# Opening in halves with identity transposes in between, token halves normed on their own load, and moved places in the per-engine step tables

## The reference, cut to what matters

```python
def swiglu(h, w_gate, w_up, w_down):
    return (jax.nn.silu(h @ w_gate) * (h @ w_up)) @ w_down

for l in range(DEPTH):          # first_block, DEPTH = 2
    f = swiglu(rms_norm(h, ffn1_pre_g[l]), ffn1_w_gate[l], ffn1_w_up[l], ffn1_w_down[l])
    h = h + 0.5 * rms_norm(f, ffn1_post_g[l])
    u = rms_norm(h, mix_pre_g[l])
    ...                         # u @ w_in, two convolutions, two attentions (C and D), gates
    h = h + rms_norm(merged @ w_o[l], mix_post_g[l])
    ...                         # second feed-forward net
for l in range(DEPTH):          # second_block
    h = hybrid_layer(h, ...)    # norm, u @ w_in, three attentions, gates, h + o @ w_out
return rms_norm_2(h, final_g)
```

## Time and profile before

| | us |
|---|---|
| median of three runs | 1720.66 |
| the profiled execution, its own time | 1720.55 |
| its span | 1718.8 |
| TensorE (PE) busy | 1657.5 (96%) |
| VectorE (DVE) busy | 1091.5 (64%) |
| ScalarE (ACT) busy | 806.2 (47%) |
| GpSimd (POOL) busy | 36.9 (2%) |
| TensorE idle in 0 to 50 | 13.8 |
| TensorE idle in 300 to 400 | 4.8 |
| TensorE idle in 1400 to 1500 | 9.6 |

### The profile page before, as it was taken

One profiled execution on the slowest core, in us unless ns is written; L12 is line 12 of the kernel. 1 busy time (PEld: TensorE's weight loads), 2 busy tenths in 40 slices (PEclk: granted clock), 3 DMA queues, 4 the chain that ended last, 5 costly groups with the idle time before them and its releaser, 6 DMA issues.

```text
span 1718.8 us, 25141 instructions
## 1 busy us (share of the span) xinstructions
PE 1657.5 (96%) x10644; PEld 1489.9 (87%) x10644; DVE 1091.5 (64%) x1269; ACT 806.2 (47%) x1071; POOL 36.9 (2%) x60
## 2 busy tenths in 40 slices
PE   6999999999999999999999999999999998899897
PEld 6999899978889999899998997788899997778776
DVE  4544578898666454655456798875754556665664
ACT  5343544555545433444345355444543446554653
POOL 0000000000000000000000000000000000000000
PEclk9999999999999999999999999999999999999999
DMA  7555454444545555555546545345555545224321
GB/s 281 189 179 197 172 220 172 166 158 148 183 179 199 194 179 189 174 203 194 182 162 221 196 170 174 131 166 194 212 187 184 193 147 163 74 91 153 118 74 49
DMA packets 54479, 292.92 MB, mean 170 GB/s; under 512 B 5712, under 2 KB 10208, under 8 KB 27232
## 3 DMA queue, kind: packets, MB, share of 16 engines
q1 hardware_dynamic: 50880, 278.94, 46.0%
q10 hardware_dynamic: 3488, 12.38, 2.0%
HBM read 290.23 MB, written 1.06 MB: 169 GB/s over the span
## 4 chain that ended last, share of the span: by engine, by line
PE 80%; DVE 9%; ACT 5%; DVEq 3%; issue 2%; DMA 1%; POOL 0%; ACTq 0%; SPq 0%; POOLq 0%
PE ps L1542 23%; PE ps L1544 23%; PE ps L1543 23%; DVE wlo L1021 3%; ACT whi L674 2%; PE ps L2005 2%; DVEq L1303 1%; DVE mix L1212 1%; PE ps L2031 1%; DMA raw<-stream 1%; PE ps L1640 1%; DVEq L1217 1%; ACT tmp L677 1%; DVE small L1304 1%; PE ps L1685 1%
## 5 line engine op out<-in xcount | busy, mean ns | idle before, releaser
L1021 DVE TENSOR_TENSOR wlo<-raw,whi 128x2048 fp32r<-128x2048 f32 (+2 forms) x270 | 603.6, 2242 | 381.3 <-ACT whi L674 372.8
L1542 PE MATMUL ps<-xhi,whi 128*128 128x256 f32 (+1 forms) x2000 | 570.1, 285 | 0.0
L1544 PE MATMUL ps<-xhi,wlo 128*128 128x256 f32 (+1 forms) x2000 | 565.8, 283 | 0.0
L1543 PE MATMUL ps<-xlo,whi 128*128 128x256 f32 (+1 forms) x2000 | 565.8, 283 | 0.0
L674 ACT ACTIVATE whi<-raw 128x2048 fp32r<-128x2048 f32 (+2 forms) x270 | 498.6, 1868 | 18.9 <-DMA raw<-stream 16.6
L1542 PEld LDWEIGHTS ps<-xhi,whi 128*128 128x128 f32 (+1 forms) x2000 | 381.9, 191 | 4.5 <-issue 0.9
L1543 PEld LDWEIGHTS ps<-xlo,whi 128*128 128x128 f32 (+1 forms) x2000 | 382.0, 191 | 3.1
L1544 PEld LDWEIGHTS ps<-xhi,wlo 128*128 128x128 f32 (+1 forms) x2000 | 381.9, 191 | 0.5
L1542 PE MATMUL ps<-whi,yar 128*128 128x512 f32 x620 | 245.6, 396 | 3.1 <-DVE yar L1529 1.6
L1543 PE MATMUL ps<-wlo,yar 128*128 128x512 f32 x620 | 241.4, 389 | 0.0
L1544 PE MATMUL ps<-whi,yar 128*128 128x512 f32 x620 | 241.0, 389 | 0.0
(11 more groups left out here) (213 smaller groups left out, 1347.3 us busy)
## 6 DMA issues: line engine op xcount, KB each, us to landing
raw<-stream SPq DMA_DIRECT2D x210, 1024.0 KB, 4.8
raw<-stream SPq DMA_DIRECT2D x88, 512.0 KB, 4.6
raw<-stream SPq DMA_DIRECT2D x22, 384.0 KB, 3.8
gpre<-pre_gain ACTq DMA_DIRECT2D x9, 512.0 KB, 4.1
gpost<-post_gain ACTq DMA_DIRECT2D x6, 512.0 KB, 5.4
mix<-cum ACTq DMA_DIRECT2D x2, 1024.0 KB, 4.7
raw<-stream SPq DMA_DIRECT2D x4, 320.0 KB, 4.3
h<-x_in SPq DMA_DIRECT2D x2, 512.0 KB, 5.9
```

The source lines that it names most:

```text
L1021: TT(wlo[:, s, 0:w], raw[:, s, 0:w], whi[:, s, 0:w].bitcast(F32), ALU.subtract).then_inc(lo_v, 1)
L1542: pe.matmul(dst, lh, rh, start=first, stop=False)
L1543: pe.matmul(dst, lh, rl, start=False, stop=False)
L1544: return pe.matmul(dst, ll, rh, start=False, stop=last)
```

## The change

In the opening: SP loads x half 0, the gain, x half 1, and chunk 0 in two halves of 1024 columns, each with a semaphore. The gain is no longer on ScalarE's queue, so the identity is first there. ScalarE and VectorE split chunk 0 by halves; ScalarE writes `xhi` of token half 0 between the two halves and that of token half 1 before it splits chunk 1; VectorE splits chunk 1 only after all four `low`. VectorE waits for each token half's own load. ScalarE issues the loads of `gpost` and of the other constants after `split(2)`. TensorE runs 18 identity transposes into bank 3 (which nothing reads) ahead of `turns(0, 0)` and 9 behind it, and `first_pair` takes the place of `token_pair` for chunks 0 and 1: the same 96 matmuls, chunk 0 first for both token halves, then chunk 1, with waits on halves.

In the tables some places are moved. Sorted, the lists change in these ways. Mixer, ScalarE: `split` 32 before `flip` 2, `split` 33 before `turn` 7 (each was behind it). Mixer, VectorE: `scores` 2 before `split` 20, and `conv` (17, 1) between the two, `weigh` 2 before `split` 21, `scores` 3 before `split` 22, `weigh` 5 and `values` 4 before `split` 27, `split` 29 behind `weigh` 6, `values` 5, `o_split` 1 and `conv` 27, `split` 30 behind `scores` 7. Mixer, TensorE: the same order as before. Hybrid, TensorE: `flip` 1 before chunk 6, `scores` 9 before `turn` 8. Hybrid, ScalarE: `split` 5 before `l_square`, `split` 6 and `l_hi` before `take` (3, 0), `split` 10 behind `o_copy` 1 (it was before `a_square`), `split` 11 behind the two `flip_copy`, `exp` 2 before `split` 12, `split` 13 before `o_copy` 4 and gate 0, `split` 14 before `o_high` 0. Hybrid, VectorE: `split` 4 before `l_norm`, `split` 5 before `l_lo`, `weigh` 6 and `split` 13 before `o_low` 0.

```diff
--- before.py
+++ after.py
@@ -162,6 +162,7 @@
 
 LANDED = landed_counts()
 GROUPS1 = 8
+WARM = 18
 
 
 COLS_V = (2, 3, 6, 7)
@@ -185,14 +186,14 @@
-    at(pe, (17.02, 19.04, 21.04, 23.04, 25.06, 27.04, 29.04, 31.04), "scores")
+    at(pe, (17.02, 19.04, 21.04, 23.04, 25.06, 27.04, 29.04, 31.3996), "scores")
-             31.55, 32.55, 33.55, 34.55, 35.55, 36.55, 37.55, 38.55, 39.55, 40.55, 41.55, 42.55, 43.55, 44.55, 45.55,
+             31.55, 31.7404, 32.55, 34.55, 35.55, 36.55, 37.55, 38.55, 39.55, 40.55, 41.55, 42.55, 43.55, 44.55, 45.55,
@@ -209,7 +210,7 @@
-             16.55, 17.55, 18.55, 19.55, 20.55, 21.55, 22.55, 23.55, 24.55, 25.55, 26.55, 27.55, 28.55, 29.55, 30.55,
+             16.55, 17.55, 18.55, 19.55, 21.05, 22.05, 23.05, 23.55, 24.55, 25.55, 26.55, 28.057, 28.55, 30.55, 31.0601,
@@ -218,7 +219,7 @@
-             19.06, 20.06, 21.06, 22.06, 23.06, 24.06, 24.1, 25.1, 25.5275, 26.08, 28.14, 29.08, 30.12, 31.08, 32.12,
+             19.06, 20.06, 21.0447, 22.06, 23.06, 24.06, 24.1, 25.1, 25.5275, 26.08, 28.14, 29.08, 30.12, 31.08, 32.12,
@@ -276,22 +277,22 @@
-    at(pe, (6.02, 6.52, 6.54, 6.56, 9.02, 9.04, 10.52, 10.54), "flip")
+    at(pe, (6.02, 6.2376, 6.54, 6.56, 9.02, 9.04, 10.52, 10.54), "flip")
-    at(pe, (7.52, 8.52, 9.5539, 10.02, 10.56, 11.02, 12.02, 12.52, 14.02, 14.52), "turn")
+    at(pe, (7.52, 8.52, 9.5539, 10.02, 10.56, 11.02, 12.02, 12.52, 14.0607, 14.52), "turn")
-    at(act, (0.91, 1.91, 2.91, 3.91, 4.6801, 5.91, 6.91, 7.91, 8.91, 9.0669, 10.91, 11.91, 12.91, 13.91, 14.4), "split", range(3, 18))
-    at(act, (1.4, 1.9, 3.4, 3.9, 4.4, 4.5105, 5.4, 5.9, 7.4, 7.9, 9.4, 9.9), "take", TAKES)
+    at(act, (0.91, 1.9031, 1.91, 2.91, 4.6801, 5.91, 6.91, 8.91, 9.0669, 9.2882, 10.91, 11.3652, 12.91, 13.91, 14.4), "split", range(3, 18))
+    at(act, (1.4, 1.9, 3.9, 4.0105, 4.0985, 4.2, 5.2, 5.7, 7.4, 7.9, 9.4, 9.9), "take", TAKES)
-    at(act, (6.6, 7.56, 9.08, 9.56, 10.06, 10.6, 11.06, 12.06, 12.56, 14.06), "exp")
-    at(act, (7.52, 8.52, 9.52, 10.02, 10.56, 11.02, 12.02, 12.52, 14.02, 14.52), "copy")
-    at(act, (7.58, 8.54, 9.58, 10.08, 10.62, 11.08, 12.08, 12.58, 14.08, 14.54), "o_copy")
+    at(act, (6.6, 7.56, 9.08, 9.56, 10.06, 10.6, 11.36, 12.06, 12.56, 14.06), "exp")
+    at(act, (7.52, 8.52, 9.52, 10.02, 10.56, 11.32, 12.02, 12.52, 14.02, 14.52), "copy")
+    at(act, (7.58, 8.54, 9.58, 10.08, 10.92, 11.38, 12.08, 12.58, 14.08, 14.54), "o_copy")
-    at(act, (10.9, 11.9, 12.9, 13.9), "gate")
-    at(act, (11.069, 13.52, 15.02), "o_high")
-    at(dve, (1.52, 2.56, 3.54, 4.52, 6.06, 7.12, 8.1, 9.06, 9.6, 10.64, 11.52, 12.6, 13.54, 14.56, 16.3), "split", range(3, 18))
+    at(act, (11.2, 11.9, 12.9, 13.9), "gate")
+    at(act, (11.369, 13.52, 15.02), "o_high")
+    at(dve, (1.52, 2.5325, 2.56, 3.54, 5.76, 7.12, 8.1, 9.06, 9.6, 10.64, 11.52, 12.6, 13.54, 14.56, 16.3), "split", range(3, 18))
@@ -304,7 +305,7 @@
-    at(dve, (11.11, 13.53, 15.03), "o_low")
+    at(dve, (11.7636, 13.53, 15.03), "o_low")
@@ -440,6 +441,9 @@
 
         landed = [sem(f"landed{i}") for i in range(SLOTS)]
         hi_ready = sem("hi_ready")
+        first_in = sem("first_in")
+        hi_half = sem("hi_half")
+        lo_half = sem("lo_half")
         lo_v = sem("lo_v")
         used = sem("used")
         cst_in_s = sem("cst_in")
@@ -598,9 +602,13 @@
         @block.sync
         def _(sp):
 
-            for t in range(NT):
-                sp.dma_start(h[:, t, :], x_in[t]).then_inc(x_in_s[t], 16)
-            for c in range(STREAM_CH):
+            sp.dma_start(h[:, 0, :], x_in[0]).then_inc(x_in_s[0], 16)
+            sp.dma_start(gpre[:, :], pre_gain[0].partition_broadcast(P)).then_inc(gpre_in, 16)
+            sp.dma_start(h[:, 1, :], x_in[1]).then_inc(x_in_s[1], 16)
+            for half in range(2):
+                cut = slice(half * CW // 2, (half + 1) * CW // 2)
+                sp.dma_start(raw[:, 0, cut], stream[LOAD[0]][:, cut]).then_inc((first_in, landed[0])[half], 16)
+            for c in range(1, STREAM_CH):
                 if c >= SLOTS:
                     sp.wait_ge(used, c - SLOTS + 1)
                 s, w = c % SLOTS, chunk_width(c)
@@ -755,19 +763,22 @@
                     hidden(g)
                     split(c + 4)
 
-            act.dma_start(gpre[:, :], pre_gain[0].partition_broadcast(P)).then_inc(gpre_in, 16)
             act.dma_start(cst[:, 0:P], cst_in[:, 0:P]).then_inc(ident_in, 16)
             for t in range(NT):
                 act.wait_ge(x_in_s[t], 16)
                 for n in range(2):
                     square(h[:, t, n * 512:(n + 1) * 512], t, n, 2)
+            for half in range(2):
+                cut = slice(half * CW // 2, (half + 1) * CW // 2)
+                if half:
+                    turned(0, 0)
+                act.wait_ge((first_in, landed[0])[half], 16)
+                A(whi[:, 0, cut], raw[:, 0, cut], ACT.Copy).then_inc((hi_half, hi_ready)[half], 1)
+            turned(0, 1)
+            split(1)
+            split(2)
             act.dma_start(gpost[:, :], post_gain[0].partition_broadcast(P)).then_inc(gpost_in, 16)
             act.dma_start(cst[:, P:CST2], cst_in[:, P:CST2]).then_inc(cst_in_s, 16)
-            split(0)
-            split(1)
-            turned(0, 0)
-            turned(0, 1)
-            split(2)
             act.dma_start(gpre[:, :], pre_gain[1].partition_broadcast(P)).then_inc(gpre_in, 16)
 
             for l in range(DEPTH):
@@ -1120,14 +1131,17 @@
                 mean_square(2 * t + 2, t, 2)
                 if t == 0:
                     dve.wait_ge(gpre_in, 16)
-                    dve.wait_ge(x_in_s[0], 16)
-                    dve.wait_ge(x_in_s[1], 16)
+                dve.wait_ge(x_in_s[t], 16)
                 normed(t, t + 1)
-            split(0)
-            split(1)
+            for half in range(2):
+                cut = slice(half * CW // 2, (half + 1) * CW // 2)
+                dve.wait_ge((hi_half, hi_ready)[half], 1)
+                TT(wlo[:, 0, cut], raw[:, 0, cut], whi[:, 0, cut].bitcast(F32),
+                   ALU.subtract).then_inc((lo_half, lo_v)[half], 1)
             for t in range(NT):
                 low(0, t, 0)
                 low(0, t, 1)
+            split(1)
             split(2)
 
             for l in range(DEPTH):
@@ -1695,9 +1709,40 @@
                         if t:
                             ins.then_inc(used, 1)
 
+            def first_part(c, t, part, x, ks, waits=()):
+
+                for w in waits:
+                    pe.wait_ge(*w)
+                for k in ks:
+                    ins = pe.matmul(ps[:, c, t * GF:(t + 1) * GF], x[:, k, t * P:(t + 1) * P],
+                                    part[:, c, k * GF:(k + 1) * GF], start=(part is whi and x is xhi and k == 0),
+                                    stop=(x is xlo and k == KD - 1))
+                return ins
+
+            def first_pair():
+
+                low_k, high_k, all_k = range(4), range(4, KD), range(KD)
+                first_part(0, 0, whi, xhi, low_k, [(hi_half, 1), (xhi_done, 1)])
+                first_part(0, 0, whi, xhi, high_k, [(hi_ready, 1), (xhi_done, 2)])
+                turns(0, 1)
+                first_part(0, 0, wlo, xhi, low_k, [(lo_half, 1)])
+                first_part(0, 0, wlo, xhi, high_k, [(lo_v, 1)])
+                first_part(0, 0, whi, xlo, all_k, [(x_ready, 2)])
+                first_part(0, 1, whi, xhi, all_k, [(xhi_done, 4)])
+                first_part(0, 1, wlo, xhi, all_k)
+                first_part(0, 1, whi, xlo, all_k, [(x_ready, 4)]).then_inc(used, 1)
+                for t in range(NT):
+                    first_part(1, t, whi, xhi, all_k, [(hi_ready, 2)])
+                    first_part(1, t, wlo, xhi, all_k, [(lo_v, 2)])
+                    ins = first_part(1, t, whi, xlo, all_k)
+                ins.then_inc(used, 1)
+
             def ffn(ch, f, X):
 
-                token_pair(ch, X, GF)
+                if X:
+                    token_pair(ch, X, GF)
+                else:
+                    first_pair()
                 ready(ch + 2)
                 pe.wait_ge(silu_done, f * NG + 1)
                 features(ch + 2, 0)
@@ -1736,7 +1781,11 @@
 
             pe.wait_ge(setup, 1)
             pe.wait_ge(ident_in, 16)
+            for n in range(WARM):
+                pe.transpose(bank(3)[:, 0:P], ident, ident)
             turns(0, 0)
+            for n in range(WARM // 2):
+                pe.transpose(bank(3)[:, 0:P], ident, ident)
             for l in range(DEPTH):
                 ch = layer1(l)
                 ffn(ch + AT_FFN1, l * 2, l * 3)
```

## The result

The changed kernel takes 1700.8 us (median of 4 runs, 1700.3 to 1702.94) against 1721.88 for the one before (4 runs, 1720.39 to 1725.74): a ratio of 0.9877, 95% interval 0.9857 to 0.9896, 21.1 us faster. The forecast was 1699.5, range 1694 to 1708. The profiled execution took 1700.73, its span is 1698.9 (1718.8 before).

The account below looks back on a forecast made before the run. The prediction took TensorE, busy 1657.5 of 1718.8 us, as the bound, so only its idle time and slow stretches counted. Seven terms summed to 21.05 us off the 1720.55 profiled, giving 1699.5 us, range 1694 to 1708.

Parts of the forecast that it names:

- forecast case: Whole kernel: the time comes as summed, 1699.5 us, its own range 1696 to 1703; chance 0.47.
- opening: Kernel start: chunk 2's product starts at 24.9 instead of 31.06, 6.1 us won.
- mixers: Both mixer layers: TensorE's waits for weigh 2, values 3 and values 6 shrink or go, 4.05 us won.
- hybrid head: Start of both hybrid layers: new 1.2 us wait at l_turn, outweighed by waits removed at the flips; 0.45 us won.
- values 1, flip 5 (a_square): Hybrid layers: split 10 no longer precedes a_square, so waits of 1.52 and 2.35 become 0.9 and 1.2; 3.5 us won.
- slowed clock behind flip 5: Hybrid layers: shorter waits leave TensorE's clock up in the slow stretches; 3.1 us won, between nothing and 5.1.
- splits 13 and 14: Hybrid layers: these splits go ahead of the gates, removing waits of 0.57 and 1.04; 3.2 us won.
- scores 9: Hybrid layers: scores 9 before turn 8 removes the 0.33 wait before the output products; 0.65 us won.
- The sum's side of the question: Opening: the sum has identity transposes warm TensorE's clock, with the higher level from 12 on.
- that rival: The lower clock stays: transposes do not warm (2.1 less), slow stretches remain (3.1 less), or both; 1701.6 to 1704.7, chance 0.25.
- the last rival: Opening and first net: the new order holds TensorE's clock down, making the kernel slower, 1727 us; chance 0.03.
- VectorE is the mixer's bound: Mixer: what turn 2 wins is waited for at turn 4 and the flips; 1702.7 us, chance 0.10.

Follow-up runs that it names:

- v3_early: The changed kernel with weigh 4 and values 3 moved ahead of a split in VectorE's mixer table; 1701.9 us (median of 4 runs).
- head_back: The changed kernel with the hybrid layer's head (splits 4 to 6, takes 2 to 7, flip 1) in the order of before; 1698.99 us (one run).
- fill_all: The changed kernel with identity transposes in five of TensorE's waits, in the mixer and hybrid layers; 1700.07 us (median of four runs).
- fill_entry: The changed kernel with 20 more identity transposes in TensorE's wait at the first hybrid layer's entry; 1699.37 us (median of 4 runs).

## Why the prediction was right

The forecast case came, 1.3 us from the median. The terms, as the prediction summed them and as the two traces give them:

```
term                            predicted   traces
opening                              6.1      5.7
mixers                               4.05     5.6
hybrid head                          0.45    -1.3
values 1, flip 5 (a_square)          3.5      4.0
slowed clock behind flip 5           3.1      2.2
splits 13 and 14                     3.2      1.5
scores 9                             0.65     1.15
not the change's                              1.1
sum                                 21.05    20.0
```

*The opening.* By its steps: the identity landed at 4.90 (estimated 5.1). x half 1 came later than kept: its square is at 8.28, not 7.79. Each step behind it on ScalarE is later by the same 0.5: the half split started at 9.89 for 9.4, both `xhi` ended at 12.06 for 11.5, the second half split at 13.0 for 12.5. That is as much as the term lacks.

*The clock there.* The sum's side of the question was right and the rule's wrong; its price, 2.1 in that rival, measured 0.95. (The longest stretch at the lower level before was 6.8 us, at 1479, not the 6.4 of the last rival; nothing hangs on it.)

*The mixers.* Turn 4 starts 1.81 and 1.78 earlier for the 1.85 said, by VectorE's idle time, as the step had it. The term behind it was mis-sized: 0.40 for turn 7's wait, 1.0 measured, since turn 5's wait of 0.20 went too, and a wait costs somewhat more than it shows. "VectorE is the mixer's bound" is now true of the next step: v3_early got nothing.

*The hybrid head.* This is the step that failed, by its sign. The new wait of 1.2 at `l_turn` came as worked out (1.19), and flip 0's 1.02 went. But in the first layer TensorE loses 1.61 up to `l_turn`, 0.4 more than the wait shows, and wins only 0.99 back up to flip 0. What the step left out is ScalarE's take (L946) ahead of the chunk behind the flips, now later: a wait of 0.55 at 1434.67, for the 0.34 that went. head_back confirms 1.05 of the 1.3. "Flip 1 finds its input" was right and worth nothing.

*a_square, flip 5.* 2.2 and 1.8 where 1.75 was said; values 1's wait fell to 1.11, not 0.9, and flip 5's to 0.60, not 1.2.

*The slowed stretches.* Right for the first layer (nothing behind flip 5) and wrong for the second, where 1.7 us are lacking from 1607 on in spite of the shorter waits. Whether a stretch comes is not settled by the wait's length, as the table above shows; a term that counts on one going can only be a chance.

*Splits 13 and 14.* The 0.57 and 1.04 went, and were half replaced: turn 7 now waits 1.04 for VectorE's weigh, which stood just behind. The step had asked for no next bound.

So the mechanisms are mostly those forecast, but that the total came so near is in part luck: four terms are too high (4.75 together), three too low (2.55), and 1.1 us no term had, 0.84 of it a late chunk in the profiled execution of before. The two profiled executions themselves differ by 19.8, the medians by 21.1.

## What to carry to other kernels

A saturated engine carries what the opening wins to the end, and in the opening the place of the small copies in a queue of long splits was worth more (4.6 of 5.7 us, up to 1.7 of it by the clock) than loading in halves or warming the clock (0.25 and 0.95). Ask of each removed wait what else reaches that point: at turn 4, 2.2 us of it were worth nothing, and at `l_turn` a wait hid the landing of a chunk that cost 1.86 once it stood bare. Where one engine idles often for a microsecond or two, compare traces instruction by instruction before reading a median: stretches of lower clock, worth 0.5 (fill_all) to 1.5 us (fill_entry) each here, come and go with unrelated edits.

## What was not expected of the hardware

Identity transposes brought TensorE's clock to its upper level (0.22 to 0.12 us apart, in the opening after 4.7 us of nothing else). Where 20 of them filled a gap of 2.35 us it stayed up in three traces of three; without them it fell in nine of eleven. The lower-clock stretches come in one size, 1.7 us of full clock lacking, or double, and the same wait of 2.2 to 2.7 us brings one in some kernels' traces and none in others. In the opening itself the profile's granted clock reads 1.00 while matmuls run at the spacing of the lower level, so there only the spacing tells.

The head of before with fill_entry's transposes would, by an estimate from single traces (1698.99 less the 1.5 of its one stretch), come to about 1697.5, if no stretch comes elsewhere as it did in fill_entry; it was not run.
